# Attention cut by token third and woven between weight slabs, in place of two attention stages

## The reference, cut to what matters

```python
# 1152 tokens: 1024 of the prompt, 8 sequences of 16 sample tokens with 1024 cached keys each
h = x + 0.5 * post1(SwiGLU_1(pre1(x)))
z = rms_norm(h) @ w_in      # attention q | k | v, recurrence inputs, gates
A = diff_attention(z_q, z_k, z_v)   # 4 heads, two softmax maps each
B = rwkv7(z_rw)                     # 8 heads of 64, a state carried from token to token
m = sigmoid(gA) * (A @ w_o_att) + sigmoid(gB) * (B @ w_o_rwkv)
h = h + post_mix(m @ w_out)
y = h + 0.5 * post2(SwiGLU_2(pre2(h)))

def diff_core(q, k, v, lam, mask):          # per head
    s = einsum(q, k) * 64 ** -0.5           # maps m = 0, 1
    pr = softmax(where(mask, s, -1e30))     # prompt: a query block sees the keys up to its own chunk
    return einsum(pr[0] - lam * pr[1], v)   # then an RMS norm over the 128 values of a head
```

## Time and profile before

| | us |
|---|---|
| median of 3 runs | 3745.56 (3742.6 to 3748.82) |
| the profiled execution | 3744.15 |
| its span, first to last instruction | 3742.4 |
| PE busy in the span | 3275.7 (88%) |
| DVE, ACT, POOL busy | 1901.0, 1428.3, 223.2 |

### The profile page before, as it was taken

How to read it: one execution, slowest core, us unless ns; L and a number is a source line. 1 busy time by engine, 2 the same in 40 slices (tenths; PEclk the granted TensorE clock), 3 DMA queues, 4 the chain that set the end, 5 groups by cost and what they waited for, 6 DMA issues and landing times. The chain is left out here.

```text
span 3742.4 us, 62771 instructions
## 1 busy us (share of the span) xinstructions
PE 3275.7 (88%) x25813; PEld 2988.8 (80%) x25813; DVE 1901.0 (51%) x3310; ACT 1428.3 (38%) x2538; POOL 223.2 (6%) x372
## 2 busy tenths in 40 slices
PE   3999999999899999979588486869999879987995
PEld 3999998898899989869455243758999779987995
DVE  3445556434646633364466522674443765456543
ACT  2435456333535633333133212553333344434432
POOL 0000111000011000011300000110000100010000
PEclk7999999999999999979799798979999989998997
DMA  4444566432457532335310343634343634463444
GB/s 155 127 144 142 154 207 194 134 100 74 134 166 223 179 103 83 111 124 173 126 51 1 136 181 117 202 118 119 86 118 104 192 107 127 144 187 109 127 126 173
DMA packets 711689, 503.13 MB, mean 134 GB/s; under 512 B 78212, under 2 KB 678000, under 8 KB 709360
## 3 DMA queue, kind: packets, MB, share of 16 engines
q1 hardware_dynamic: 684416, 407.07, 36.0%
q0 software_dynamic: 26992, 92.10, 6.8%
HBM read 423.50 MB, written 75.56 MB: 133 GB/s over the span
## 5 line engine op out<-in xcount | busy, mean ns | idle before, releaser
L547 DVE TENSOR_TENSOR fr_wlo<-fr_raw,fr_whi 128x512 fp32r<-128x512 f32 (+1 forms) x660 | 449.2, 681 | 866.0 <-ACT fr_whi L455 864.8
L455 ACT ACTIVATE fr_whi<-fr_raw 128x512 fp32r<-128x512 f32 (+1 forms) x660 | 408.6, 622 | 840.4 <-PE ps L684 798.8
L920 DVE TENSOR_TENSOR bk_wlo<-bk_raw,bk_whi 128x512 fp32r<-128x512 f32 x504 | 341.6, 678 | 571.8 <-ACT bk_whi L832 571.2
L832 ACT ACTIVATE bk_whi<-bk_raw 128x512 fp32r<-128x512 f32 x504 | 311.8, 619 | 579.2 <-PE ps L1073 551.6
L684 PE MATMUL ps<-fr_hidhi,fr_whi 128*128 128x384 f32 x1536 | 531.0, 346 | 0.0
L684 PE MATMUL ps<-fr_hidlo,fr_whi 128*128 128x384 f32 x1536 | 514.9, 335 | 0.0
L684 PE MATMUL ps<-fr_hidhi,fr_wlo 128*128 128x384 f32 x1536 | 514.9, 335 | 0.0
L1073 PE MATMUL ps<-bk_xahi,bk_whi 128*128 128x384 f32 x1248 | 438.5, 351 | 29.5 <-DVE bk_xalo L992 20.8
L1073 PE MATMUL ps<-bk_xalo,bk_whi 128*128 128x384 f32 x1248 | 423.5, 339 | 0.0
L1073 PE MATMUL ps<-bk_xahi,bk_wlo 128*128 128x384 f32 x1248 | 423.3, 339 | 0.0
L684 PE MATMUL ps<-fr_xahi,fr_whi 128*128 128x384 f32 x1056 | 373.0, 353 | 14.0 <-DVE fr_xalo L616 12.6
(11 more groups left out here) (383 smaller groups left out, 4713.1 us busy)
## 6 DMA issues: line engine op xcount, KB each, us to landing
fr_raw<-in_ffn_w_in_dram SPq DMA_DIRECT2D x264, 256.0 KB, 2.9
bk_raw<-in_ffn_w_in_dram SPq DMA_DIRECT2D x264, 256.0 KB, 2.9
fr_raw<-in_w_in_dram SPq DMA_DIRECT2D x252, 256.0 KB, 2.9
fr_raw<-in_ffn_w_out_dram SPq DMA_DIRECT2D x120, 256.0 KB, 2.7
bk_raw<-in_ffn_w_out_dram SPq DMA_DIRECT2D x120, 256.0 KB, 2.6
zT_scratch<-fr_zo POOLq DMA_DIRECT2D x126, 192.0 KB, 2.7
sa_kc<-in_cache_att_k_dram SPq DMA_DIRECT2D x8, 2048.0 KB, 11.7
sa_vc<-in_cache_att_v_dram SPq DMA_DIRECT2D x8, 2048.0 KB, 7.2
```

The source lines that it names most:

```text
L455: act.activation(w["hi"][:, s % RING, 0:x.n], raw[:, s % RING, 0:x.n], ACT.Copy).then_inc(whi, 1)
L547: dve.tensor_tensor(w["lo"][:, s % RING, 0:x.n], raw[:, s % RING, 0:x.n], w["hi"][:, s % RING, 0:x.n].bitcast(F32), ALU.subtract).then_inc ...
L832: act.activation(w["hi"][:, s % RING, 0:x.n], raw[:, s % RING, 0:x.n], ACT.Copy).then_inc(whi, 1)
L920: dve.tensor_tensor(w["lo"][:, s % RING, 0:x.n], raw[:, s % RING, 0:x.n], w["hi"][:, s % RING, 0:x.n].bitcast(F32), ALU.subtract).then_inc ...
```

## The change

The two attention stages are gone. Three things replace them.

`attention` is the prompt attention of one third as a stream, begun when the recurrence of the same third has ended, with the same memory (`area`) as the recurrence: 4 steps for loads, 18 for rotating, transposing and storing, 4 for loads of keys and values, 4 steps per unit (12 units for T = 0 and 1, 8 for T = 2), 15 for the last unit and the norm. T = 0 and 1 stand in front, T = 2 in back. The two maps of a unit now take turns in the same two PSUM banks, two steps apart.

`sample_attention` becomes a stream of 85 steps in back, 8 steps per sequence, and its value matmuls go by head into four column groups of PE (32 rows of output each) instead of one matmul of 512 columns for all heads.

The recurrence's tiles start every 12 steps instead of every 16 and so overlap. Its streams begin at slots 226 and 480 of front and 0 of back; attention begins at 391 and 645 of front and at 201 of back, the samples at 274 of back. The attention of T = 1 ends at step 734 of front, sixteen past the 718 that the weave walks (714 slots and 4), so that its end runs without slabs. The sum over the four lambda vectors moves to load_inputs. The load of the last third's mixer outputs in back moves from slot 348 to 367 (`takes`).

```diff
-MIXER_AT = 10
+MIXER_AT = 0
...
-        r_sync, r_pool, r_pool_start, r_pool_end, r_act, r_dve, r_pe, own_done = recurrence(t, S, sb, sem, [0, 1], z_ready)
+        r_sync, r_pool, r_pool_start, r_pool_end, r_act, r_dve, r_pe, own_done, r_done = recurrence(
+            t, S, area, sem, [0, 1], lambda eng, T: z_ready(eng, T, ZRT), lambda eng, T: a_done(eng, T - 1) if T else None)
+        a_steps, a_sync, a_pool, a_pool_end, a_act, a_dve, a_pe, a_done = attention(
+            t, S, area, sem, [0, 1], lambda eng, T: z_ready(eng, T, ZRT + ZR), lambda eng, T: r_done(eng, T))
+        begins = [mixed]
+        for T in range(2):
+            begins += [begins[-1] + mixer_end(T), begins[-1] + mixer_end(T) + a_steps(T)]
...
-LORA_STEPS, TILE_STEPS = LOAD_STEPS + 5, 16
+LORA_STEPS, TILE_STEPS, TILE_EVERY = LOAD_STEPS + 5, 16, 12
...
+    def on_act(act, T):
...
+                if k in (2, 4):
+                    m = k // 2 - 1
+                    act.wait_ge(peaked, 2 * u + m + 1)
...
+                    act.activation(ex[:, m, 0:N], ps[:, BANK0:BANK0 + 2, :].rearrange("p b c -> p (b c)")[:, 0:N], ACT.Exp,
...
+    def on_pe(pe, T):
...
+        for step in range(UNIT_STEPS * len(units) + 5):
+            for i, (h, b) in enumerate(units):
+                k, u = step - UNIT_STEPS * i, base + i
...
+                if k in (0, 2):
+                    m = k // 2
...
+                    if 2 * u + m >= 1:
+                        pe.wait_ge(exped, 2 * u + m)
+                    rows_m = slice(64 * m, 64 * m + 64)
+                    for j, (a, e) in enumerate(cols(b)):
+                        pe.matmul(bank(j)[:, 0:e - a], qk[rows_m, h, at:at + P], kh[rows_m, h % 2, a:e], start=True, stop=e != N)
+                    ins = pe.matmul(bank(j)[:, e - a - CHUNK:e - a], S["mask"][:, 0:P], S["mask"][:, P:P + CHUNK], start=False, stop=True)
+                    ins.then_inc(scored, 1)
+                elif k == 5 or (k == 6 and b >= 4):
+                    g = k - 5
+                    pe.wait_ge(mixed, 2 * u + 2)
...
+                elif k == 7:
...
+                    pe.wait_ge(flipped_out, group_base(T, i + 1))
+                    for q in range(b + 1):
+                        ins = pe.matmul(bank(3)[:, 0:P], vh[:, h % 2, q], awT[:, q], start=q == 0, stop=q == b)
...
+                    for p in (2 * (k - 12), 2 * (k - 12) + 1):
+                        no = PIECES * n + p
+                        pe.wait_ge(v_in[no % 3], 16 * (no // 3 + 1))
+                        for i in range(2):
+                            for h in range(HEADS):
+                                at_w = (2 * p + i) * 64 + h * NQ
+                                ins = pe.matmul(bank(2)[32 * h:32 * h + 32, 0:P], awT[:, at_w:at_w + 2 * NQ], vc[:, no % 3, i, h * P:(h + 1) * P],
...
         front(nc, t, S)
-        prompt_attention(nc, t, S)
-        sample_attention(nc, t, S)
         back(nc, t, S)
```

More of the change, by code:

```diff
@@ L394, in _ @@
                 load(x)
-            plan.weave(body, [(mixed[n], r_sync(sp, n)) for n in range(2)])
+            plan.weave(body, mixers(sp, r_sync, a_sync))
         @block.gpsimd
@@ L446, in _ @@
             r_pool_end(pool)
+            a_pool_end(pool)
         @block.scalar
@@ L757, in along @@
                 if T + 1 < THIRDS:
-                    out.append((first_down[T] + 10, take(T + 1)))
+                    out.append((takes[T + 1], take(T + 1)))
                 out.append((finals[T], final(T)))
@@ L805, in body @@
                         pool.dma_start(resid, feature_tiles(t["res1"], *tokens(T))).then_inc(back_in, 16)
-                    if T + 1 < THIRDS and i == first_down[T] + 1:
+                    if T + 1 < THIRDS and i == takes[T + 1] - 6:
                         load_o(T + 1)
@@ L912, in _ @@
                 split(s)
-            plan.weave(body, along(take, mix, final, lambda T: r_act(act, T)))
+            plan.weave(body, along(take, mix, final, mixers(act, r_act, a_act, s_act)))
         @block.vector
@@ L1041, in _ @@
             own = Chain(dve, own_done)
-            plan.weave(body, along(take, mix, final, lambda T: r_dve(dve, T, own)))
+            plan.weave(body, along(take, mix, final, mixers(dve, r_dve, a_dve, s_dve, own)))
         @block.tensor
@@ L1573 @@
+            plan.weave(body, along(take, mix, final, mixers(pe, r_pe, a_pe, s_pe)))
 CHUNKS = SEQ // CHUNK
@@ L1591, in mixer_steps, with tiles_at, mixer_end, recurrence @@
 def mixer_steps(T):
-    chunks = LORA_STEPS + RT * TILE_STEPS + 6
+    chunks = LORA_STEPS + ALL_TILES + 6
     out = chunks + sum(chunk_steps(PER_THIRD * T + k) for k in range(PER_THIRD)) + 2
     return chunks, out
-def recurrence(t, S, sb, sem, thirds, z_ready):
+def tiles_at(step):
+    return [(c, step - TILE_EVERY * c) for c in range(RT) if 0 <= step - TILE_EVERY * c < TILE_STEPS]
+def mixer_end(T):
+    return mixer_steps(T)[1] + (32 if T == THIRDS - 1 else 24)
+def recurrence(t, S, area, sem, thirds, z_ready, area_ready):
     ps = S["ps"]
-    area = sb("area", [P, 11264])
     G = (RT, CHUNK)
@@ L1715, in on_sync @@
             load_tiles(c)
-            yield from rest(TILE_STEPS)
-        yield from rest(begin[0] - LOAD_STEPS - LORA_STEPS - (RT - 1) * TILE_STEPS - 4)
+            yield from rest(TILE_EVERY)
+        yield from rest(begin[0] - LOAD_STEPS - LORA_STEPS - (RT - 1) * TILE_EVERY - 4)
         for q in range(2):
@@ L1883, in keep @@
+        yield from rest(begin[0] - LORA_STEPS - ALL_TILES)
         def keep(ch, p, dst, frm):
```

1258 lines of the change are left out of this document (678 added, 580 removed).

## The result

| | before | after |
|---|---|---|
| median of 4 runs, us | 3747.19 (3742.6 to 3751.1) | 3677.83 (3672.49 to 3680.85) |
| ratio, 95% interval | | 0.9815 [0.9803, 0.9826] |
| span of the profiled execution, us | 3742.4 | 3679.0 |
| PE busy, us | 3275.7 | 3263.2 |
| mean granted clock | 0.943 | 0.936 |

The changed kernel is 69 us faster, not 147 as forecast. The time lies inside the range that was given, 3505 to 3690, but near its upper end: the span came out 83.1 us above the sum of 3595.9. The place of each of these 83 us can be read from the trace, since the slabs are numbered alike in both kernels: from the first matmul of a slab to that of a later one, before and after.

The account below looks back on a forecast made before the run. PE bounds the slab stretches; in the 531.1 us between, engines wait in turn. 3742.4 - 531.1 + 15.3 + 35 + 258.8 + 74 + 0 + 1.5 = 3595.9 span, 3599 us forecast; range 3505 to 3690.

Parts of the forecast that it names:

- What bounds, and what goes: Between front's and back's slabs no engine is full; the 531.1 us of attention stages there go.
- PE's work between slabs, 258.8: Attention work put between slabs: 39.8 (T = 0), 56.8 (T = 1), 66.2 (T = 2), 96 (samples), in us.
- the rival of the column groups: Samples in back: column groups do not help at 128 columns, values 8.3 instead of 2.8, time 3643; chance 0.05.
- Exponentials behind sigmoids, 24: Front's slots 682 to 713: PE waits 1.5 us in each of 16 steps for exponentials behind sigmoids on ACT.
- The hand-over, 15.3: From the store of the last attention rows to back's first slab: 15.3 us, kept from the kernel before.
- The tail, 35: Rest of T = 1 behind front's last slab, uncovered by slabs: 35 us (30 to 45), 3 for a lower clock.
- The recurrence's packing, 0 (-25 to +30): Recurrence tiles packed in 12 slots instead of 16: set to 0 us, -25 to +30.
- the 50 or 55 of a chain of 10 us per unit: Back's gap without slabs: five units of T = 2, chains of 10 us each, let it grow to 50 or 55.
- Loads, 18: PE waits 6 us per third for attention's loads, 18 us in all.
- Waits of the samples, 16: Samples in back: PE waits 2 us per sequence, mostly at the mix, 16 us in all.
- late splits: Rival: ACT and DVE late, splits of later slabs fall behind, 90 us more, 3690; chance 0.12 for 3650 to 3740.
- the convoy: Rival: streams hold each other up, each exchange paid in full; 3775 at 1.1 us per wait; slower by over 0.2%: 0.05.

Follow-up runs that it names:

- the fourth experiment: Recurrence of T = 2 begun with back's first slab again (MIXER_AT 10 instead of 0), against the changed kernel: 3681.47 us, ratio 0.9825 to the kernel before.

## Why the prediction was right in kind and wrong in size

**What bounds, and what goes:** right. The 531 us went, and what came back came back at slabs that cover most of it: PE's busy time is within 13 us of before.

**PE's work between slabs, 258.8:** right where it could be read alone. Values of the samples are 512 instructions of 278 ns that overlap, 19.1 us in all, 2.4 per sequence (taken: 2.8), so the rival of the column groups is out. In front's last slots some 6 us more than forecast remain (below).

```profile
L2481 PE MATMUL ps<-bk_area 128*32 128x128 f32 x512 | 19.1, 278 | 11.5 <-DMA bk_area<-in_cache_att_v_dram 11.5
```

**Exponentials behind sigmoids, 24:** right in place and cause (22.6 us of waits, 24.6 of idle time), with some luck in the size: 13 waits of 1.7 us and not 16 of 1.5, since none fell into the time at the lower clock. Wrong is what was left out. The prediction named a fall of PE's clock only as something that would make it wrong, and gave it no price but the 3 us in the tail. That is the first step that failed: all of PE's work in slots 682 to 713 was summed at the full clock, though the forecast itself put an idle time into every second step there, and the earlier trace rows already showed clocks of 0.87 and 0.60 in stretches in which PE waits. Some 20 of the 30.5 us of this term are that, and by the same sum 3 more in slots 645 to 682, at a clock of 0.97. PE's idle time over slots 645 to 713 is 30.3, as forecast (24 + 6). The 6 or 7 that are left are PE's own work there, 56.8 in the sum; which price was too low no run shows.

**The hand-over, 15.3:** the second step that failed, and the larger: 41.0 us, 25.7 more than the sum had. It was copied from a place where SP held the last store and no stream stood ahead of the first slab; the change altered both. The diff of begins (MIXER_AT to 0) and the engine of the store could be read in the order. 9.5 us are POOL's end, mostly its drain; 16 stand behind back's first load, where the recurrence's first steps are ahead of the slab; the fourth experiment took 12.8 of these away, without a gain in the whole. **The tail, 35:** 39.4, in its bounds.

**The recurrence's packing, 0 (-25 to +30), and T = 2:** together 15.8 low, and which of the two it is stays open. For the packing: undoing it in back saved 11.6 and 14.7 us from front's last slab to slot 386 in two profiles, and moving the attention out of the gap without undoing it (the fourth experiment) saved 1; but ten slots and twelve put the streams beside other slabs, so the one is no clean measure of the other. For the gap: from slot 10 to 229, the recurrence and the attention's preparation, back grew by 15.2 us where the sum has 15.1 (rotation 5.8, transposes 3.3, loads 6), and from slot 229 to 274, the units and the norm, by 82.8 where it has 67.1. The gap itself took 82.6 us at a clock of 0.59, not the 50 or 55 of a chain of 10 us per unit; here too the clock was left out. In front, where the sum was 8.3 us too high, the same packing was kept throughout.

**Loads, 18:** near. PE waits three times, 14.3 us in all, for the rotation's table (L2175). **Waits of the samples, 16:** these were put to the mix; they were at the values' transfers (11.5) and the keys' copies (11.8), 25.0 in all: the wrong reason, and 9 short.

**Rivals:** late splits did not come about (PE and its weight loads waited 2 us in all for a split, L581 and L968), nor did the convoy. (The convoy's 3775 at 1.1 us is 3771 by its own numbers: 3599 - 74 + 224 x 1.1.)

## What to carry to other kernels

Price the clock with the wait: where a forecast puts an idle gap into every other step of PE, look up the granted clock of a stretch with such gaps and charge the work around them at it; shifting one stream by one step, so that two heavy pieces of ACT fall into different steps, gave most of both back. A constant taken over from the old kernel (a hand-over, a load's landing) holds only with the same engine, queue and neighbours on either side; when the change alters one of them, work it out anew. And ask in which step a transfer is requested against the step that needs it: one step earlier was worth 12 us.

## What the runs showed of the hardware

After a stage whose last DMA is POOL's, the trace of the changed kernel holds a DRAIN of POOL of 7.0 us behind the landing of the store (4.8 us at the end of front before, 4.2 at the end of back), in which all engines wait at the barrier. With the last store on SP, SP's drain is 0.01 us; POOL's still takes 6.9, but earlier, under other work. Stores of 192 KB by SP landed 1.8 us after issue, the one of 768 KB by POOL 4.0. A function on ACT starts 0.01 us behind the load of its table (1940.51 + 1.28, 1941.80). Matmuls that nobody reads, put where PE waits, raised the granted clock (0.86 to 0.93, and 0.59 to 0.87 in the gap); in the gap they made the stretch shorter, 82.6 to 75.3 us.
